# Half rows of the mixing two steps earlier between turned blocks, its last weights apart, VectorE's rests one step later

## The chip, the core and the metric

The kernel runs on one core of a Trainium2 chip. The metric is the device time in microseconds (us) of one execution. TensorE (PE in the profile) multiplies and transposes into the accumulation memory (PSUM), ScalarE (ACT) and VectorE (DVE) read it, GpSimd (POOL) and SyncE's queue (SP) stand beside them. TensorE works at one of two clock levels, 1.2 or 2.4 GHz; the profile shows the granted clock as a share of the higher one.

## The reference, cut to what matters

One layer of one model is followed by one layer of another, on 1024 tokens of width 1024, in float32. The change lies in the second layer, where a stick-breaking attention runs over 8 heads and the output of two attentions is mixed:

```python
oa = chunked_rel_attention(qa, ka, va, rel_bias)       # rows2[:, :, 0:512] in the kernel
ob = stick_breaking_attention(qb, kb, vb)              # rows2[:, :, 512:1024]
mixed = jnp.concatenate([rms_norm(oa) * g_a, rms_norm(ob) * g_b], axis=-1) @ w_out
x = x + gate_mix[:, None, :] * mixed
# stick_breaking_attention, for each block of 128 queries:
log_beta = jax.nn.log_sigmoid(logits)
log_keep = jnp.where(strict, jax.nn.log_sigmoid(-logits), 0.0)
log_tail = lax.cumsum(log_keep, axis=3, reverse=True) - log_keep
weights = jnp.where(strict, jnp.exp(log_beta + log_tail), 0.0)
outs.append(jnp.einsum("bhqk,bkhd->bqhd", weights, v))
```

The first half of the mixing, `rms_norm(oa) * g_a` with the upper 512 rows of `w_out`, needs only the attention that is already done; it can run beside the second attention.

## The kernel before

Every float32 product is made of three matmuls of rounded operands: high x high, low x high, high x low (`passes`, L818 to L820). So each operand exists as a high part, which ScalarE writes by a copy, and a low part, the **rest**, which VectorE writes by a subtraction.

The stick-breaking attention runs in 96 **steps** (`NS`), 24 for each of four pairs of heads. A step is one head, one block of 128 queries and up to four blocks of keys. Each engine has its own loop over `s`, and the order in it is written by hand:

- TensorE, step s: `turn3(s-2)` turns the weights (L1400), `outputs3(s-4)` multiplies them with v (L1416, L1418), `jobs3(s)` gives two slices of the q, k, v products of a coming pair (steps 0 to 71), `beside3(s)` follows, and in odd steps `scores3(s+1)` (L1385, L1391) gives the logits of the next two steps.
- ScalarE, step s: `turned_hi(s-3)` (wt_hi), `signs(s)` (keep, stick), the high part of a product that ended in step s-1 and the high part of the next weights (`stick_weight_hi`), `beside3(s)`.
- VectorE, step s: `tails(s-1)` (the scan L2452 over keep, the product L2456 with stick), `turned_lo3(s-3)` (wt_lo, L2461), the rest of that product (`job_lo`), `beside3(s)`, and last the rest of the next weights (`stick_weight_lo`, L2080).

`turn3(z)` waits for the tail of z and for the wt_lo two steps back. A product's half ends every fourth step, at s % 4 = 3; its rest stands in the step after. The table `BANK3` says which of the two banks of `pd[:, 0]` a product uses.

The mixing runs in `beside3`. **Blocks** 0 to 7 (`turn_mixed`) turn the first attention's output into `actT`, 128 columns by 512 rows each; blocks 8 to 11 do so for the first half of the rows of the second. **Half rows** 0 to 15 (`first_half_row`) multiply them with the first half of the weights, 12 matmuls each (row r = n // 2, half h = n % 2). VectorE's `first_half_sum(n)` scales the result (L2494, which frees the bank, `c0_free`) and adds it to the residual (L2497). The residual, `rows3`, comes back from DRAM by one DMA (L674) that SP issues when `outputs3(71)` has freed its place; the first sum waits for it (`mid_in`). ScalarE and VectorE split the eight tiles of mixing weights in steps 72 to 75 and 94 to 97 (`mix_weight_hi`, L1901, and `mix_weight_lo`, L2485). The second half of the mixing (`second_row`) starts when VectorE has left the loop.

Before, TensorE has blocks 0 to 7 in steps 74 to 77, two in each, half rows 0 to 15 in steps 78 to 93, and blocks 8 to 11 in steps 94 to 97; the other two engines follow one step later.

## Time and profile before

| | us |
|---|---|
| median of 3 timed runs | 2663.93 (2662.77 to 2664.50) |
| the profiled execution | 2653.37 |
| its span, from the first to the last instruction | 2651.6 |
| TensorE busy in the span | 2557.0 (96%) |
| VectorE busy | 1529.8 (58%) |
| ScalarE busy | 789.4 (30%) |
| TensorE's share of the chain that ended last | 87% |
| mean granted clock | 0.973 |

In the profile a row of the timeline tells the start, the busy time, engine and line, operation, output and inputs with their sizes, and the count; in square brackets stand the idle time before it and what ended that. Matmuls overlap, so what one costs is the distance from its start to the next start. The third attention lies between 1522 and 1856 us.

### The profile page before, as it was taken

The numbers are of one execution on the slowest core, as the hardware profiler recorded it, in microseconds if no ns is written. First come the engines' busy times: TensorE is split into PE (matmuls) and PEld (weight loads), VectorE is DVE, ScalarE is ACT, GpSimd is POOL, SyncE is SP. The second block draws the span as 40 slices with busy tenths as digits, with TensorE's granted clock in tenths as the row PEclk, the third lists the DMA queues.
The fourth block names the chain that finished last, engine by engine and source line by source line (L and its number), as shares of the span: only waits on it lengthen the run. The fifth ranks groups of instructions, "written<-read, shape, count | busy, mean of one in ns | idle before, by whom it ended". The sixth has DMA issues, their size and how long they took to land.

```text
span 2651.6 us, 32495 instructions
## 1 busy us (share of the span) xinstructions
PE 2557.0 (96%) x12496; PEld 2112.1 (80%) x12496; DVE 1529.8 (58%) x2345; ACT 789.4 (30%) x1353; POOL 188.4 (7%) x94
## 2 busy tenths in 40 slices
PE   7999999999999999998999999989999999999998
PEld 6777787888888888787888877777788888888886
DVE  6668265444344437646454577778566555646466
ACT  2245041111011102535433355544532121212122
POOL 6303300000000000001222200000000000000000
PEclk9996999999999999998999999979999999999999
DMA  3403613223232323113110001021012121202011
GB/s 121 37 9 81 79 33 93 93 77 94 86 93 77 94 86 117 31 42 116 32 42 27 25 17 33 17 96 38 19 56 64 33 63 32 63 32 63 32 56 72
DMA packets 201576, 157.05 MB, mean 59 GB/s; under 512 B 56184, under 2 KB 176512, under 8 KB 201472
## 3 DMA queue, kind: packets, MB, share of 16 engines
q1 hardware_dynamic: 183344, 124.94, 16.5%
q10 hardware_dynamic: 18128, 30.71, 4.4%
q8 instruction: 67, 1.10, 0.2%
q14 instruction: 37, 0.30, 0.0%
HBM read 147.23 MB, written 11.56 MB: 60 GB/s over the span
## 4 chain that ended last, share of the span: by engine, by line
PE 87%; DVE 6%; ACT 2%; issue 2%; DMA 2%; SPq 1%; POOL 1%; ACTq 0%; DVEq 0%; PEldq 0%; POOLq 0%
PE pd L818 25%; PE pd L820 25%; PE pd L819 25%; PE pt L1338 1%; PE pd L1385 1%; DMA raw<-in_w_out 1%; PE pd L1307 1%; PE pt L1400 1%; PE pt L818 1%; PE pt L1416 1%; PE pt L1355 1%; PE pt L838 1%; PE pt L1418 1%; PE pt L820 1%; PE pt L819 1%
## 5 line engine op out<-in xcount | busy, mean ns | idle before, releaser
L818 PE MATMUL pd<-actT_hi,st_hi 128*128 128x512 f32 x1872 | 749.3, 400 | 7.0 <-DVE st_lo L2233 3.6
L820 PE MATMUL pd<-actT_hi,st_lo 128*128 128x512 f32 x1872 | 733.4, 392 | 0.0
L819 PE MATMUL pd<-actT_lo,st_hi 128*128 128x512 f32 x1872 | 732.6, 391 | 0.0
L818 PEld LDWEIGHTS pd<-actT_hi,st_hi 128*128 128x128 f32 x1872 | 354.0, 189 | 76.9 <-ACT evac L1573 3.9
L820 PEld LDWEIGHTS pd<-actT_hi,st_lo 128*128 128x128 f32 x1872 | 353.2, 189 | 75.2
L819 PEld LDWEIGHTS pd<-actT_lo,st_hi 128*128 128x128 f32 x1872 | 354.4, 189 | 66.6
L818 PE MATMUL pd<-mv_hi,hid_hi 128*128 128x512 f32 x864 | 337.3, 390 | 3.5 <-DVE acc L2547 1.5
L819 PE MATMUL pd<-mv_lo,hid_hi 128*128 128x512 f32 x864 | 336.5, 389 | 0.0
L820 PE MATMUL pd<-mv_hi,hid_lo 128*128 128x512 f32 x864 | 336.3, 389 | 0.0
L1704 ACT ACTIVATE mv_hi<-raw 128x1024 fp32r<-128x1024 f32 x54 | 55.9, 1056 | 603.6 <-PE pd L820 478.1
L1573 ACT ACTIVATE evac<-pd 128x1024 f32<-128x1024 f32 x76 | 77.9, 1024 | 451.9 <-PE pd L820 451.9
L2196 DVE TENSOR_TENSOR acc<-acc,pd 128x1024 f32<-128x1024 f32 x72 | 87.9, 1221 | 190.9 <-PE pd L820 190.8
L818 PEld LDWEIGHTS pd<-mv_hi,hid_hi 128*128 128x128 f32 x864 | 162.2, 188 | 39.2 <-DVE acc L2547 3.2
L820 PEld LDWEIGHTS pd<-mv_hi,hid_lo 128*128 128x128 f32 x864 | 162.2, 188 | 33.8
L819 PEld LDWEIGHTS pd<-mv_lo,hid_hi 128*128 128x128 f32 x864 | 162.2, 188 | 33.3
L2233 DVE TENSOR_TENSOR st_lo<-raw,st_hi 128x1024 fp32r<-128x1024 f32 (+1 forms) x83 | 103.5, 1249 | 117.4 <-ACT st_hi L1704 111.2
L757 POOL TENSOR_TENSOR st_hi<-raw,ones 128x1024 fp32r<-128x1024 f32 x27 | 67.7, 2507 | 1186.9 <-PE pd L820 1170.3
L2546 DVE TENSOR_TENSOR gated<-pd,row_b 128x1024 f32<-128x1024 f32 x48 | 58.8, 1225 | 104.2 <-PE pd L820 103.5
L2606 DVE TENSOR_SCALAR cv<-evac,cw,cb 128x1024 f32<-128x1024 f32 x44 | 35.7, 811 | 119.0 <-ACT evac L1573 117.8
L1704 ACT ACTIVATE st_hi<-raw 128x1024 fp32r<-128x1024 f32 (+1 forms) x83 | 89.0, 1075 | 51.3 <-DMA raw<-in_w_ff 19.6
L2452 DVE TENSOR_TENSOR_SCAN tail<-keep,tail 128x512 f32<-128x512 f32 (+3 forms) x96 | 97.1, 1011 | 7.6 <-ACT keep L1874 7.1
L2233 DVE TENSOR_TENSOR mv_lo<-raw,mv_hi 128x1024 fp32r<-128x1024 f32 x54 | 65.0, 1223 | 60.4 <-ACT mv_hi L1704 59.1
(340 smaller groups left out, 3763.0 us busy)
## 6 DMA issues: line engine op xcount, KB each, us to landing
raw<-in_w_ff SPq DMA_DIRECT2D x64, 512.0 KB, 4.0
ada_raw<-in_w_ada ACTq DMA_DIRECT2D x64, 384.0 KB, 3.2
raw<-in_w_up SPq DMA_DIRECT2D x44, 512.0 KB, 3.8
raw<-in_w_in SPq DMA_DIRECT2D x30, 512.0 KB, 3.7
raw<-in_w_down SPq DMA_DIRECT2D x22, 512.0 KB, 3.4
acc<-in_x SPq DMA_DIRECT2D x16, 512.0 KB, 8.8
raw<-in_w_out SPq DMA_DIRECT2D x12, 512.0 KB, 3.4
raw<-in_w_ple_gate SPq DMA_DIRECT2D x8, 512.0 KB, 3.8
```

The costliest lines, as they stand in the source:

```text
L757: pool.tensor_tensor(hi.rearrange("p (k n) -> p k n", n=P), src.rearrange("p (k n) -> p k n", n=P), ones[:, :].unsqueeze(1).to_broadcast([ ...
L818: pe.matmul(out_ap, a_hi, b_hi, start=start, stop=False, skip_group_check=check)
L819: pe.matmul(out_ap, a_hi, b_lo, start=False, stop=False, skip_group_check=check)
L820: return pe.matmul(out_ap, a_lo, b_hi, start=False, stop=stop, skip_group_check=check)
L838: last = pe.transpose(pt[:, job % 4, r * P:(r + 1) * P], src[:, half * 4 + r, kt * P:(kt + 1) * P], ident[:, :])
L1573: act.activation(buf[:, t % 2, :], pd[:, t % 2, :], func, **kw).then_inc(t_free, 1)
L1704: act.activation(hi, src, ACT.Copy).then_inc(split_hi, 1)
L2196: return dve.tensor_tensor(acc[:, r, :], acc[:, r, :], pdr(r), ALU.add)
L2233: dve.tensor_tensor(lo, src, hi.bitcast(F32), ALU.subtract).then_inc(w_ready, 1)
L2452: link(dve.tensor_tensor_scan(tail[:, f % 2, c1 - n:c1][:, ::-1], kept, kept, tail[:, f % 2, c1:c1 + 1], ALU.mult, ALU.min))
L2546: link(dve.tensor_tensor(gt[:, :], pdr(r), row_gate[:, :], ALU.mult))
L2606: link(dve.tensor_scalar(y, u, cw[:, 2, ds(f, 1)], cb[:, ds(f, 1)], ALU.mult, ALU.add))
```

## The change

A table `mix_steps(s)` says which half rows ("r") and blocks ("b") a step has, and all three engines read it. Blocks 0 to 3 stay in steps 74 and 75. Half rows 0 to 15 stand in steps 76 to 91, and blocks 4 to 7 behind half rows 0 to 3, one in each. Blocks 8 to 11 stand in steps 92 to 95. `mix_bank` puts half rows 0 to 3 in bank 0 and blocks 4 to 7 in bank 1; the waits on `c0_free` and `tp_lo` follow from that. The last four mixing weights are split in steps 92, 93, 95 and 96, behind the step's block on ScalarE and VectorE. The rests of q and k products and of the attention's next weights stand one step later on VectorE.

```diff
+        def mix_steps(s):
+            if 74 <= s < 76:
+                return [("b", 2 * (s - 74)), ("b", 2 * (s - 74) + 1)]
+            if 76 <= s < 80:
+                return [("r", s - 76), ("b", s - 72)]
+            if 80 <= s < 92:
+                return [("r", s - 76)]
+            return [("b", s - 84)] if 92 <= s < 96 else []
+        def mix_bank(kind, n):
+            return 1 if kind == "b" and 4 <= n < 8 else 0 if kind == "r" and n < 4 else n % 2
...
             def first_half_row(n):
                 r, h = n // 2, n % 2
+                bank = mix_bank("r", n)
                 if n == 0:
                     pe.wait_ge(w_ready, UN["out2"] + 4)
+                    pe.wait_ge(tp_lo, TPJ["o2"] + 4)
+                elif n == 5:
                     pe.wait_ge(tp_lo, TPJ["o2"] + 8)
-                if n >= 2:
-                    pe.wait_ge(c0_free, n - 1)
+                else:
+                    pe.wait_ge(c0_free, n if n < 5 else n - 1)
...
-                if 94 <= s < 98:
-                    mix_weight_hi(s - 90)
-                if 95 <= s < 99:
-                    b = s - 87
-                    mixed_hi(b, pd[:, 0, b % 2 * HB:(b % 2 + 1) * HB])
+                if s in (92, 93, 95, 96):
+                    mix_weight_hi((92, 93, 95, 96).index(s) + 4)
...
-                    for q, e, kind, half in stick_ends(s - 1):
-                        job_lo(0, 4 * NJ1 + NJ2 * q, att2[q % 2], [(e, kind, half)], q)
+                    for q, e, kind, half in stick_ends(s - 1) + stick_ends(s - 2):
+                        if (kind == "T") == ((q, e, kind, half) in stick_ends(s - 1)):
+                            job_lo(0, 4 * NJ1 + NJ2 * q, att2[q % 2], [(e, kind, half)], q)
...
-                    for q, e, kind, half in stick_ends(s - 1):
+                    for q, e, kind, half in stick_ends(s - 2):
                         if kind != "T" and half:
                             stick_weight_lo(next_unit(q, e))
```

**VectorE, steps 16 and 17** (tail, stick: the tail and its product; k_lo2b: the rest of the k product; rsq: the inverse roots, 14 rows of which the first or last ones stand; st_lo: the rest of the next weights). Before, in two pieces:

```order
1355 L2461 TENSOR_TENSOR wt_lo<-pt,wt_hi 128x512
1356 L2097 TENSOR_TENSOR k_lo2b<-pd,k_hi2b 128x512
1357 L2467 TENSOR_SCALAR rsq_v<-ssq 128x8
1358 L2468 TENSOR_SCALAR rsq_a<-rsq_v 128x8
...
1370 L2473 TENSOR_TENSOR rsq_a<-rsq_a,rsq_t 128x8
1371 L2080 TENSOR_TENSOR st_lo<-raw,st_hi 128x1024
1372 L2452 SCALAR_TENSOR_TENSOR tail<-keep,tail 128x512
1373 L2456 TENSOR_TENSOR stick<-stick,tail 128x512
1374 L2461 TENSOR_TENSOR wt_lo<-pt,wt_hi 128x256
```

Now:

```order
1355 L2476 TENSOR_TENSOR wt_lo<-pt,wt_hi 128x512
1356 L2482 TENSOR_SCALAR rsq_v<-ssq 128x8
1357 L2483 TENSOR_SCALAR rsq_a<-rsq_v 128x8
...
1369 L2488 TENSOR_TENSOR rsq_a<-rsq_a,rsq_t 128x8
1370 L2467 SCALAR_TENSOR_TENSOR tail<-keep,tail 128x512
1371 L2471 TENSOR_TENSOR stick<-stick,tail 128x512
1372 L2476 TENSOR_TENSOR wt_lo<-pt,wt_hi 128x256
1373 L2112 TENSOR_TENSOR k_lo2b<-pd,k_hi2b 128x512
1374 L2095 TENSOR_TENSOR st_lo<-raw,st_hi 128x1024
```

The tail and the wt_lo that stood behind roots, k_lo2b and st_lo now stand directly behind the roots, ahead of the other two.

**TensorE, step 76 and the start of step 77** (L1400, now L1414: turned weights; ident,rows: blocks; w_hi, w_lo with actT: a half row; k, q: scores). Before:

```order
5278 L1400 MATMUL pt<-ident,stick 128x128 x2
5279 L1416 MATMUL pt<-v2b,wt_hi 128x128
5280 L1418 MATMUL pt<-v2b,wt_lo 128x64
5281 L1429 MATMUL pd<-ident,rows_56 128x128 x8
5282 L1400 MATMUL pt<-ident,stick 128x128 x2
5283 L1416 MATMUL pt<-v2b,wt_hi 128x128
5284 L1418 MATMUL pt<-v2b,wt_lo 128x64
5285 L1429 MATMUL pd<-ident,rows_56 128x128 x8
5286 L1385 MATMUL pd<-k_hi2b,q_hi2b 128x512 x2
```

Now:

```order
5278 L1414 MATMUL pt<-ident,stick 128x128 x2
5279 L1430 MATMUL pt<-v2b,wt_hi 128x128
5280 L1432 MATMUL pt<-v2b,wt_lo 128x64
5281 L832 MATMUL pd<-w_hi,actT_hi 128x512
5282 L833 MATMUL pd<-w_lo,actT_hi 128x512
...
5292 L834 MATMUL pd<-w_hi,actT_lo 128x512
5293 L1443 MATMUL pd<-ident,rows_56 128x128 x4
5294 L1414 MATMUL pt<-ident,stick 128x128 x2
5295 L1430 MATMUL pt<-v2b,wt_hi 128x128
5296 L1432 MATMUL pt<-v2b,wt_lo 128x64
5297 L832 MATMUL pd<-w_hi,actT_hi 128x512
```

Where two blocks of four transposes stood (x8), half row 0 stands with block 4 behind it, and half row 1 follows in the next step.

**VectorE, around the end of the half rows** (half_gated: the first operation of a sum; w_lo: a mixing weight's rest; actT_lo: a block's rest). Before, steps 94 and 95, with row 15's sum at the head:

```order
1675 L2494 SCALAR_TENSOR_TENSOR half_gated<-pd,rsq_a,mix_gate 128x512
1676 L2497 TENSOR_TENSOR rows_57<-rows_57,half_gated 128x512
1677 L2485 SCALAR_TENSOR_TENSOR w_lo<-raw,gab,w_hi 128x1024
1678 L2452 SCALAR_TENSOR_TENSOR tail<-keep,tail 128x512
1679 L2456 TENSOR_TENSOR stick<-stick,tail 128x512
1680 L2461 TENSOR_TENSOR wt_lo<-pt,wt_hi 128x512
1681 L2485 SCALAR_TENSOR_TENSOR w_lo<-raw,gab,w_hi 128x1024
1682 L2479 TENSOR_TENSOR actT_lo<-pd,actT_hi 128x512
1683 L2452 SCALAR_TENSOR_TENSOR tail<-keep,tail 128x512
```

Now, from row 15's sum in step 92:

```order
1671 L2509 SCALAR_TENSOR_TENSOR half_gated<-pd,rsq_a,mix_gate 128x512
1672 L2512 TENSOR_TENSOR rows_57<-rows_57,half_gated 128x512
1673 L2500 SCALAR_TENSOR_TENSOR w_lo<-raw,gab,w_hi 128x1024
1674 L2467 SCALAR_TENSOR_TENSOR tail<-keep,tail 128x512
1675 L2471 TENSOR_TENSOR stick<-stick,tail 128x512
1676 L2476 TENSOR_TENSOR wt_lo<-pt,wt_hi 128x384
1677 L2494 TENSOR_TENSOR actT_lo<-pd,actT_hi 128x512
1678 L2500 SCALAR_TENSOR_TENSOR w_lo<-raw,gab,w_hi 128x1024
1679 L2467 SCALAR_TENSOR_TENSOR tail<-keep,tail 128x512
1680 L2471 TENSOR_TENSOR stick<-stick,tail 128x512
1681 L2476 TENSOR_TENSOR wt_lo<-pt,wt_hi 128x384
1682 L2494 TENSOR_TENSOR actT_lo<-pd,actT_hi 128x512
```

The same weights and blocks follow row 15's sum; they now stand in steps with two more tails behind them, and the block comes ahead of the weight.

## Rows read from the trace of the kernel before

**Rows 1.** Stretches: us, busy PE, PEld, DVE, ACT, POOL (instructions), granted clock, DMA, GB/s

```profile
1574.40:1577.80 3.40, 3.40 (x14) 2.92 (x13) 3.37 (x6) 1.14 (x4) 0.00 (x0) 0.50 0.00 0
...
1745.00:1766.80 21.80, 16.46 (x72) 14.09 (x72) 15.52 (x27) 12.27 (x27) 0.00 (x0) 0.50 0.71 266
...
1766.80:1772.30 5.50, 5.44 (x13) 4.21 (x14) 2.26 (x3) 0.44 (x1) 0.00 (x0) 0.50 0.00 0
...
1772.40:1840.30 67.90, 67.90 (x403) 55.42 (x401) 56.42 (x80) 25.21 (x59) 0.00 (x0) 1.00 0.00 1
```

**Rows 2.** TensorE's timeline, turned weights of steps 10, 18, 42 and 43

```profile
1546.21 0.63 PE L1400 MATMUL pt<-ident,stick 128*128 128x128 f32 x4 [0.87 <-DVE wt_lo L2461]
...
1572.89 0.63 PE L1400 MATMUL pt<-ident,stick 128*128 128x128 f32 x4 [2.85 <-DVE wt_lo L2461]
...
1647.42 0.63 PE L1400 MATMUL pt<-ident,stick 128*128 128x128 f32 x4 [0.36 <-DVE wt_lo L2461]
...
1649.73 0.60 PE L1400 MATMUL pt<-ident,stick 128*128 128x128 f32 x4
```

**Rows 3.** VectorE's timeline, step 16

```profile
1565.83 0.69 DVE L2097 TENSOR_TENSOR k_lo2b<-pd,k_hi2b 128x512 fp32r<-128x512 f32 x1 [2.48 <-ACT k_hi2b L1609]
...
1569.26 1.22 DVE L2080 TENSOR_TENSOR st_lo<-raw,st_hi 128x1024 fp32r<-128x1024 f32 x1
...
1570.41 1.28 DVE L2452 TENSOR_TENSOR_SCAN tail<-keep,tail 128x512 f32<-128x512 f32 x1
```

**Rows 4.** TensorE's timeline, steps 78 to 82

```profile
1766.86 0.77 PE L818 MATMUL pd<-w_hi,actT_hi 128*128 128x512 f32 x1 [1.51 <-DVE actT_lo L2479]
...
1772.11 0.61 PE L1400 MATMUL pt<-ident,stick 128*128 128x128 f32 x3
...
1772.93 0.47 PE L818 MATMUL pd<-w_hi,actT_hi 128*128 128x512 f32 x1
...
1777.02 0.62 PE L1400 MATMUL pt<-ident,stick 128*128 128x128 f32 x4
...
1778.07 0.48 PE L818 MATMUL pd<-w_hi,actT_hi 128*128 128x512 f32 x1
...
1780.91 0.60 PE L1400 MATMUL pt<-ident,stick 128*128 128x128 f32 x4
...
1785.35 0.66 PE L1400 MATMUL pt<-ident,stick 128*128 128x128 f32 x4
```

**Rows 5.** SP's timeline and the DMA view (count, size, us to landing), residual

```profile
1749.93 0.38 SPq L674 DMA_DIRECT2D rows<-x_mid  x1
...
rows<-x_mid SPq DMA_DIRECT2D x1, 4096.0 KB, 14.0
```

**Rows 6.** VectorE's timeline, rests of blocks 2, 3 and the first sum

```profile
1755.70 1.29 DVE L2479 TENSOR_TENSOR actT_lo<-pd,actT_hi 128x512 fp32r<-128x512 f32 x2 [2.87 <-ACT actT_hi L1894]
...
1772.41 0.75 DVE L2494 SCALAR_TENSOR_TENSOR half_gated<-pd,rsq_a,mix_gate 128x512 f32<-128x512 f32 x1 [3.31 <-issue]
```

**Rows 7.** TensorE's timeline, steps 92 and 94, first row of the second half

```profile
1828.24 0.52 PE L1400 MATMUL pt<-ident,stick 128*128 128x128 f32 x3
...
1837.22 0.66 PE L1400 MATMUL pt<-ident,stick 128*128 128x128 f32 x4
...
1838.30 0.66 PE L1429 MATMUL pd<-ident,rows 128*128 128x128 f32 x4
...
1856.04 0.76 PE L818 MATMUL pd<-w_hi,actT_hi 128*128 128x512 f32 x1 [1.41 <-DVEq L2541]
```

**Rows 8.** VectorE's timeline, steps 92, 94 and 95

```profile
1830.95 0.55 DVE L2461 TENSOR_TENSOR wt_lo<-pt,wt_hi 128x384 fp32r<-128x384 f32 x1
...
1839.55 1.28 DVE L2485 SCALAR_TENSOR_TENSOR w_lo<-raw,gab,w_hi 128x1024 fp32r<-128x1024 f32 x1 [1.64 <-ACT w_hi L1901]
...
1840.75 1.28 DVE L2452 TENSOR_TENSOR_SCAN tail<-keep,tail 128x512 f32<-128x512 f32 x1
...
1842.67 0.69 DVE L2461 TENSOR_TENSOR wt_lo<-pt,wt_hi 128x512 fp32r<-128x512 f32 x1
```

More of the change, by code:

```diff
@@ L1433, in first_half_row @@
                 r, h = n // 2, n % 2
+                bank = mix_bank("r", n)
                 if n == 0:
                     pe.wait_ge(w_ready, UN["out2"] + 4)
+                    pe.wait_ge(tp_lo, TPJ["o2"] + 4)
+                elif n == 5:
                     pe.wait_ge(tp_lo, TPJ["o2"] + 8)
-                if n >= 2:
-                    pe.wait_ge(c0_free, n - 1)
+                else:
+                    pe.wait_ge(c0_free, n if n < 5 else n - 1)
                 for j in range(4):
-                    last = passes(pd[:, 0, h * HB:(h + 1) * HB], actT_hi[:, j, r * P:(r + 1) * P],
+                    last = passes(pd[:, 0, bank * HB:(bank + 1) * HB], actT_hi[:, j, r * P:(r + 1) * P],
                                   actT_lo[:, j, r * P:(r + 1) * P], w0_hi[:, j, h * HB:(h + 1) * HB],
@@ L1445, in beside3 @@
             def beside3(s):
-                if 74 <= s < 78:
-                    for b in range(2 * (s - 74), 2 * (s - 73)):
-                        if b < 2:
-                            pe.wait_ge(jb_lo, 4 * NJ1 + NL2 * 8)
-                        else:
-                            pe.wait_ge(tp_lo, TPJ["o2"] + b - 1)
-                        turn_mixed(b, pd[:, 0, b % 2 * HB:(b % 2 + 1) * HB])
-                elif 78 <= s < 94:
-                    first_half_row(s - 78)
-                elif 94 <= s < 98:
-                    b = s - 86
-                    if b == 8:
+                for kind, n in mix_steps(s):
+                    bank = mix_bank(kind, n)
+                    if kind == "r":
+                        first_half_row(n)
+                        continue
+                    if n < 2:
+                        pe.wait_ge(jb_lo, 4 * NJ1 + NL2 * 8)
+                    elif n == 4:
+                        pe.wait_ge(tp_lo, TPJ["o2"] + 4)
+                    elif 4 < n < 8:
+                        pe.wait_ge(tp_lo, TPJ["o2"] + n)
+                    elif n == 8:
                         pe.wait_ge(o_rows, 14)
                         pe.wait_ge(c0_free, 16)
-                    elif b >= 10:
-                        pe.wait_ge(tp_lo, TPJ["o2"] + b - 1)
-                    turn_mixed(b, pd[:, 0, b % 2 * HB:(b % 2 + 1) * HB])
+                    else:
+                        pe.wait_ge(tp_lo, TPJ["o2"] + n - 1)
+                    turn_mixed(n, pd[:, 0, bank * HB:(bank + 1) * HB])
             scores3(0)
@@ L1915, in beside3 @@
                     mix_weight_hi(s - 72)
-                if 75 <= s < 79:
-                    for b in range(2 * (s - 75), 2 * (s - 74)):
-                        mixed_hi(b, pd[:, 0, b % 2 * HB:(b % 2 + 1) * HB])
+                for kind, n in mix_steps(s - 1):
+                    bank = mix_bank(kind, n)
+                    if kind == "b":
+                        mixed_hi(n, pd[:, 0, bank * HB:(bank + 1) * HB])
                 if 88 <= s < 92:
@@ L2504, in beside3 @@
                     mix_weight_lo(s - 72)
-                if 75 <= s < 79:
-                    for b in range(2 * (s - 75), 2 * (s - 74)):
-                        mixed_lo(b, pd[:, 0, b % 2 * HB:(b % 2 + 1) * HB])
-                if 79 <= s < 95:
-                    if s == 79:
-                        dve.wait_ge(mix_gate_in, 16)
-                    first_half_sum(s - 79)
+                for kind, n in mix_steps(s - 1):
+                    bank = mix_bank(kind, n)
+                    if kind == "b":
+                        mixed_lo(n, pd[:, 0, bank * HB:(bank + 1) * HB])
+                    else:
+                        if n == 0:
+                            dve.wait_ge(mix_gate_in, 16)
+                        first_half_sum(n)
                 if s == 99:
```

10 lines of the change are left out of this document (3 added, 7 removed).

## The prediction

> **What bounds the kernel now.** I read the page first (its table stands above): TensorE is busy for 96% of the span and carries 87% of the chain that ended last, so only two things can move the end: idle time of TensorE, and time in which it works at the lower of its two clock levels, 1.2 instead of 2.4 GHz. Then I read the third attention, steps 0 to 99 at 1522 to 1856 us, by stretches with the granted clock, and looked up TensorE's gaps in its timeline. The reader is to see three kinds of loss. First, in steps 0 to 71 TensorE waits only now and then for VectorE, for the low part of the turned weights (wt_lo) [rows 2]; just before, VectorE had itself waited 2.48 us for ScalarE's high part of a product, with the next tail standing behind it in its order [rows 3]. Second, 1745 to 1766.8 is granted 0.50 and TensorE works 16.46 of 21.8 us: turned blocks without rows [rows 1, 4]. Third, the light steps at the end, where VectorE is full: 16.5 us without a gap from its fifth weight rest to the first row of the second half [rows 7, 8]. In between, 1772.4 to 1840.3, TensorE is full at full clock [rows 1]: there two half rows earlier are no gain in themselves, they only move work.
>
> **Part A, VectorE's rests one step later.** Nothing is added: 12 rests and 7 weight rests change places with one tail and one wt_lo. What it buys is the wait: in the step after a product ends, ScalarE has the keep and stick activations ahead of the high part. Worst is step 16, where the inverse roots stand there too. Before: wait to 1565.83, rest and roots to 1569.26, weight rest to 1570.41, and only then the tail; TensorE, ready at 1572.89 - 2.85 = 1570.04, starts at 1572.89 [rows 2, 3], and 1574.4 to 1577.8 is granted 0.50 [rows 1]. After: VectorE is free at 1565.83 - 2.48 = 1563.35 and starts with the roots (1569.26 - 1565.83 less the rest's 0.6 = 2.8) to 1566.2. ScalarE's keep for the tail is there, since it precedes the high part that came at 1565.8. Tail and product 1.92 (1840.75 to 1842.67 [rows 8]) to 1568.1, wt_lo 0.4 (tail, product, wt_lo and the hand-over are 2.48, 1570.41 to 1572.89) to 1568.5: TensorE waits for nothing at 1570.04. Rest 0.6, weight 1.15, tail 1.92, wt_lo 0.4 follow, to 1572.5; TensorE wants them one step later, 1570.04 + 2.3 (step 42, the same step of the next pair, 1647.42 to 1649.73 [rows 2]) = 1572.35, so some 0.2 is late next. The clock's dip follows this stall and should go with it; 3.4 us at half clock cost 1.7. Gain 2.85 - 0.2 + 1.7 = 4.35. The gap of 0.87 stands three times, once in each pair (steps 10, 34, 58) [rows 2] (there the first of them); there only rest and weight rest are in the way, and what is late next is the tail one step on, between 0 and 0.4. I take 0.75 of each, 2.25. The 0.36 of step 42 gives 0.3. The weights' loads leave SP's queue one step later too; they are wanted some eight steps later, so that costs nothing. **A = 6.9 us gained**; bounds 0 (the tail is late by as much) and 2.85 + 1.7 + 2.6 + 0.36 = 7.5.
>
> **Part B, rows 0 to 5 and blocks 4 to 7, up to step 82.** Steps 74 and 75 are as before. Row 0 needs the rests of blocks 0 to 3; their end is 1755.70 + 1.29 = 1757.0 [rows 6]. It runs at half clock as before, 5.25 us [rows 4], to 1762.3, block 4 (some 0.5: 0.66 less its overlap [rows 7]) and the small products of step 77 to 1763.3. Row 1 goes to the same bank and waits for VectorE's first sum, and this waits for the rows of x that come back from DRAM: issued at 1749.93 + 14.0 = 1763.9 [rows 5]. Before, that landing was hidden, row 0 ended at 1772.11; **now it ends last**. The sum's first operation 0.75 [rows 6], so row 1 starts at 1764.85, after a wait of 1.5. Then at full clock: row 1 and scores 4.09 (step 79 before is 4.91, less the 0.82 of its small products), block 0.5 = 4.6; step 78: 0.82 + 2.84 (a row alone, 1778.07 to 1780.91) + 0.5 = 4.15; step 79: 4.91 + 0.5 and some 0.4 of waiting for the sum in the single bank = 5.8; steps 80 and 81: 8.33 as 1777.02 to 1785.35 [rows 4]. Step 82 starts at 1764.85 + 22.9 = 1787.7 with six rows done, before at 1785.35 with four. Two rows are 5.7, the lag is 2.3: gain 3.4. Against it: the stretch around row 1 has a wait of 1.5 with 1 us of small work on either side, like the 2.85 with small work ahead of the dip of 1574.4 [rows 1, 2]. I take a dip of that size, 3.4 us at half clock, -1.7. **B = 1.7 us gained**, bounds 3.4 and, with the clock low to the end of row 3, -7.7 (below).
>
> By the Trainium skill ("TensorE: Matmul & The Clock Gate", section "Wait — 56ns, not 53.3ns?") matmuls of 512 columns start every 426.7 ns at 1.2 GHz and every 215.7 ns at 2.4. The first agrees with the trace (12 in 5.25 us). By the second two rows would be worth 24 x 0.2157 = 5.2 us instead of 5.7, and B half a microsecond less; the trace has 0.237 per matmul of a row, and the sum goes by that.
>
> **Part C, the last steps.** From the start of step 92 to the first row of the second half it takes 1856.04 - 1828.24 = 27.8 us before, of which rows 14 and 15 are 5.7: 22.1 [rows 7]. Now the light steps are 92 to 99 instead of 94 to 99. VectorE's first weight rest comes 2.3 us after the start of its step (1839.55 against 1837.22) [rows 7, 8], then its 16.5 us without a gap, and in them now two more tails (2 x 1.92) and two more wt_lo (2 x 0.5 [rows 8]): 2.3 + 16.5 + 4.85 = 23.7. The order of weights and blocks changes nothing in that sum; weights 6 and 7 land long before steps 95 and 96. The last outputs, which run at half clock here, end some 0.5 later than that by my estimate: 24.2. **C = -2.1 us.** Moving the rows forward takes them from under VectorE's cover here; that is where part of B goes back. Bounds: -2.1 - 1, if the weights wait behind ScalarE, and 0 if VectorE is not full in steps 92 and 93.
>
> **Sum**: 6.9 + 1.7 - 2.1 = 6.5, say 6.6 us gained by the profiled execution: 2653.37 - 6.6 = 2646.8. That execution is 10.6 us below the median of the timed runs, 2663.93; no row says where they spend more, so I take the difference over: 2657.3.
>
> **Rivals.** *The stall only moves on* (A falls): VectorE has as much to do as before, and if the tail of the next step is late by what was won, A is 0 to 1 and B + C = -0.4: 2663.5. For it: ScalarE still holds wt_hi behind weight and high part. Against it: VectorE idles 2.48 us right at the worst place [rows 3]. 0.20. *The clock stays low over the first rows* (slower): four rows share one bank, row 1 waits for the landing, and if TensorE is not granted 2.4 GHz before row 4, rows 1 to 3 cost 3 x (5.25 - 2.84) = 7.2 more, their blocks 3 x 0.5 = 1.5, scores and small products 2.4: 11.1 in place of 1.7, so 2657.3 + 9.4 = 2666.7; together with the first rival 2673. It decides at the end of row 0: before, the clock came back only when row 0 had run alone for 5.5 us [rows 1, 4]. Against it: row 0 and block 4 are 5.7 us again. 0.08. *No dip at all*: B is 3.4, and one of the short dips behind the stage (1.7) may fail to come, as they hang on stalls of 2 to 3 us: 2657.3 - 3.4 = 2653.9. 0.14. My forecast, with 0.58, has a range of its own of 2654.5 to 2660.5.
>
> **How the numbers follow.** What a measurement of this kernel tells from no change is 0.2%, 5.3 us: below 2658.6 is faster. Of the forecast three quarters lie below, 0.43; with 0.14 of the third rival 0.57 for faster. The rest of the forecast, the first rival and half of the second make 0.39 for no difference, and 0.04 is left for slower. Range 2653 to 2665: it leaves out the deeper ends of the second and third rival.
>
> **What would show it.** A: no gap at step 18, a granted clock of 1.00 at 1574 to 1578, and step 20 some 4 us earlier; wrong if the gap stands at step 19. B: row 1 starting right after the landing of the rows of x, about 15 us after their issue, and the granted clock back at row 1 or 2; wrong if rows 2 and 3 run in 5 us each. C: some 24 us from step 92 to the first row of the second half, VectorE without a gap; wrong if it is 22. The forecast as a whole is wrong if the landing comes much later than 14 us, or if the timed runs stall elsewhere than the profiled one.

## The result and the profile after

The changed kernel's timed runs have a median of 2647.48 us (20 runs), the kernel before beside them 2663.90 (20 runs). The ratio is 0.9946, with a 95% interval of 0.9932 to 0.9961: 14.4 us faster, 10.4 to 18.1. The forecast was 2657.3 with a range of 2653 to 2665, so the direction is right and the time lies below the range. A second measurement of the same kernel (10 runs) gave 0.9967 (0.9949 to 0.9985), 8.8 us. Weighting the two by their intervals gives 0.9954, 12.2 us (about 9 to 15). The profiled execution took 2644.14 us, its span 2642.3. One timed run of the kernel pool_weights below took 3198.04 us, some 20% more than its others, and stands in no ratio.

The page of the changed kernel: busy time of the engines, and the chain that ended last by engine. The answering numbers of before stand in its table (TensorE 2557.0, 96%, and 87% of the chain).

```profile
PE 2558.7 (97%) x12496; PEld 2112.3 (80%) x12496; DVE 1530.6 (58%) x2345; ACT 788.6 (30%) x1353; POOL 189.5 (7%) x94
...
PE 89%; DVE 5%; ACT 2%; DMA 2%; issue 2%; POOL 1%; SPq 0%; ACTq 0%; DVEq 0%; PEldq 0%; POOLq 0%
```

The span is 9.3 us shorter, but that is not the measure of the change: the changed kernel's execution starts the third attention 3.8 us later (step 8 at 1543.48 against 1539.67), where nothing was changed, because its clock was low for 88.7 us of the first 410 against 68.2. So I measure by stretches between starts on TensorE. Each number is a difference of two starts in the timeline; some of the rows that enter are shown here or in [rows 4, 7]. (12.1 us are gained in these stretches and 3.8 lost ahead of them; the last 1.0 of the 9.3 lies behind them, where the kernel before has a dip of the clock of 3.4 us at 1919.1 that this trace lacks. It stands in eight of the fourteen traces read here, with either order.)

| us | before | after | difference |
|---|---|---|---|
| A: step 8 to step 72 | 198.63 | 189.21 | 9.4 gained |
| B: step 72 to step 83 | 51.21 | 51.53, with two rows (5.7) more | 5.4 gained |
| step 83 to step 92 | 38.73 | 38.73 | 0 |
| C: step 92 to the second half's first row | 27.80 | 24.77, with two rows (5.7) fewer | 2.7 lost |
| sum | 316.37 | 304.24 | 12.1 gained |

The forecasts were A 6.9, B 1.7, C -2.1. The order's three places look as follows.

**A.** TensorE's timeline of the changed kernel at the places of [rows 2], the turned weights of steps 10, 18, 42 and 43, and of step 11:

```profile
1549.07 0.66 PE L1414 MATMUL pt<-ident,stick 128*128 128x128 f32 x4
...
1552.30 0.63 PE L1414 MATMUL pt<-ident,stick 128*128 128x128 f32 x4 [0.28 <-DVE wt_lo L2476]
...
1572.98 0.66 PE L1414 MATMUL pt<-ident,stick 128*128 128x128 f32 x4
...
1643.66 0.66 PE L1414 MATMUL pt<-ident,stick 128*128 128x128 f32 x4
...
1645.99 0.60 PE L1414 MATMUL pt<-ident,stick 128*128 128x128 f32 x4
```

VectorE's timeline there in steps 16 and 17, to set beside [rows 3]:

```profile
1565.32 0.69 DVE L2476 TENSOR_TENSOR wt_lo<-pt,wt_hi 128x512 fp32r<-128x512 f32 x1
...
1568.75 1.28 DVE L2467 TENSOR_TENSOR_SCAN tail<-keep,tail 128x512 f32<-128x512 f32 x1
...
1571.01 0.68 DVE L2112 TENSOR_TENSOR k_lo2b<-pd,k_hi2b 128x512 fp32r<-128x512 f32 x1
...
1571.61 1.22 DVE L2095 TENSOR_TENSOR st_lo<-raw,st_hi 128x1024 fp32r<-128x1024 f32 x1
```

No wait is left in front of the four steps. One has come, 0.28 us in front of step 11: the tail behind the moved rest is late there, as the forecast had allowed for. VectorE goes from the turned weights straight to the roots, which end at 1568.75, takes the tail, and only then k_lo2b, whose high part has long been there: the 2.48 us of waiting of [rows 3] are gone. Part of A is seen in full only on TensorE's weight loads (PEld); of the matmul rows behind them two carry a wait, of 0.31 and 0.32 us. The weight loads' timeline in the kernel before shows five such waits; two of them, in steps 29 and 37:

```profile
1608.08 0.19 PEld L1416 LDWEIGHTS pt<-v2b,wt_hi 128*128 128x128 f32 x1 [0.55 <-DVE rows L2535]
...
1632.71 0.19 PEld L1416 LDWEIGHTS pt<-v2b,wt_hi 128*128 128x128 f32 x1 [0.46 <-DVE rows L2535]
```

Here the outputs wait for VectorE's add of the heads' rows (L2535), which frees their bank. The changed kernel has none of the five.

**B.** The answers to [rows 4 to 6]. TensorE's timeline of the changed kernel, at half row 0, block 4, half rows 1 and 3:

```profile
1751.55 0.47 PE L832 MATMUL pd<-w_hi,actT_hi 128*128 128x512 f32 x1 [2.32 <-DVE actT_lo L2494]
...
1755.97 0.60 PE L1443 MATMUL pd<-ident,rows 128*128 128x128 f32 x4
...
1757.07 0.50 PE L832 MATMUL pd<-w_hi,actT_hi 128*128 128x512 f32 x1
...
1767.18 0.50 PE L832 MATMUL pd<-w_hi,actT_hi 128*128 128x512 f32 x1 [0.72 <-DVE half_gated L2509]
```

SP's timeline, the issue of the residual's load:

```profile
1743.17 0.38 SPq L688 DMA_DIRECT2D rows<-x_mid  x1
```

The DMA view (issues, KB, us to landing):

```profile
rows<-x_mid SPq DMA_DIRECT2D x1, 4096.0 KB, 13.0
```

VectorE's timeline, its first sum:

```profile
1756.26 0.75 DVE L2509 SCALAR_TENSOR_TENSOR half_gated<-pd,rsq_a,mix_gate 128x512 f32<-128x512 f32 x1 [2.67 <-PE pd L834]
```

**The clock.** Stretches of the changed kernel, columns as in [rows 1]:

```profile
1574.40:1577.80 3.40, 3.40 (x21) 2.63 (x21) 3.37 (x6) 1.78 (x4) 0.00 (x0) 1.00 0.47 142
1741.80:1748.60 6.80, 4.88 (x24) 3.98 (x22) 5.34 (x10) 2.56 (x5) 0.00 (x0) 0.50 0.62 210
1748.70:1752.00 3.30, 0.98 (x7) 0.86 (x8) 1.88 (x4) 2.90 (x7) 0.00 (x0) 1.00 1.02 421
1752.10:1755.50 3.40, 3.40 (x9) 2.67 (x8) 1.46 (x3) 0.00 (x0) 0.00 (x0) 0.50 1.03 413
1755.60:1830.50 74.90, 72.33 (x434) 59.00 (x433) 62.39 (x89) 31.04 (x70) 0.00 (x0) 1.00 0.06 20
1830.60:1851.10 20.50, 15.45 (x64) 13.96 (x63) 15.89 (x33) 7.19 (x12) 0.00 (x0) 0.50 0.33 104
```

At 1574.4 the granted clock is 1.00, it was 0.50. Around the first rows it is low for 6.8 + 3.4 = 10.2 us, before for 21.8 + 5.5 = 27.3 [rows 1]; row 0 runs at half clock only until 1755.5 and takes 4.42 us (5.25 before). Row 1 follows 1.1 us later, behind block 4 and the small products. Its matmul row carries no wait (its weight load 0.25 us, for the sum), since the load landed at 1743.17 + 13.0 = 1756.2, just when row 0 was done: VectorE's first sum had waited for TensorE last, not for the load.

**C.** TensorE's timeline of the changed kernel, turned weights of steps 92, 95 and 97 and the second half's first row, as in [rows 7]:

```profile
1822.95 0.52 PE L1414 MATMUL pt<-ident,stick 128*128 128x128 f32 x3
...
1833.26 1.09 PE L1414 MATMUL pt<-ident,stick 128*128 128x128 f32 x4 [2.37 <-DVE wt_lo L2476]
...
1840.68 1.08 PE L1414 MATMUL pt<-ident,stick 128*128 128x128 f32 x4 [1.68 <-DVE wt_lo L2476]
...
1847.72 0.76 PE L832 MATMUL pd<-w_hi,actT_hi 128*128 128x512 f32 x1 [1.00 <-DVEq L2555]
```

VectorE's timeline, its first weight rest and tail, and the last two wt_lo, as in [rows 8]:

```profile
1825.26 1.28 DVE L2500 SCALAR_TENSOR_TENSOR w_lo<-raw,gab,w_hi 128x1024 fp32r<-128x1024 f32 x1 [1.88 <-ACT w_hi L1918]
...
1826.46 1.28 DVE L2467 TENSOR_TENSOR_SCAN tail<-keep,tail 128x512 f32<-128x512 f32 x1
...
1842.25 0.68 DVE L2476 TENSOR_TENSOR wt_lo<-pt,wt_hi 128x512 fp32r<-128x512 f32 x1
...
1844.04 0.69 DVE L2476 TENSOR_TENSOR wt_lo<-pt,wt_hi 128x512 fp32r<-128x512 f32 x1 [1.11 <-ACT wt_hi L1901]
```

VectorE has its first weight rest at 1825.26, 2.3 us after the start of step 92, and works from there to 1842.9 without a gap, with TensorE waiting for its wt_lo. Ahead of its last wt_lo it waits 1.11 us for ScalarE; in the kernel before VectorE has no gap here.

### The profile page after: what moved, and what is told of

It is laid out like the page before. It is cut to its first block, busy times and chain, and to the rows that moved or that the text cites. A ratio compares the mean times of both kernels' runs of the same rounds, so it can differ in the third digit from the quotient of the medians.

```text
span 2642.3 us, 32495 instructions
## 1 busy us (share of the span) xinstructions
PE 2558.7 (97%) x12496; PEld 2112.3 (80%) x12496; DVE 1530.6 (58%) x2345; ACT 788.6 (30%) x1353; POOL 189.5 (7%) x94
## 4 chain that ended last, share of the span: by engine, by line
PE 89%; DVE 5%; ACT 2%; DMA 2%; issue 2%; POOL 1%; SPq 0%; ACTq 0%; DVEq 0%; PEldq 0%; POOLq 0%
PE pd L832 26%; PE pd L834 25%; PE pd L833 25%; PE pt L1352 1%; PE pd L1399 1%; PE pt L1414 1%; PE pt L1430 1%; PE pd L1321 1%; PE pt L832 1%; DMA raw<-in_w_out 1%; PE pt L1369 1%; PE pt L1432 1%; PE pt L852 1%; PE pt L833 1%; PE pt L834 1%
```

## The experiments

**The theory**: A, B and C as measured above, and they add up. **The rivals**: the surplus over the forecast lies outside these steps (in the timed runs' clock), or in one of the parts alone. Since single times of one kernel scatter by some 7 us (standard deviation of the changed kernel's 20), a mean over 12 is good to 2 us, over 6 to 3; the stretches between steps repeat to 0.1 us where the clock is the same. So each run is read by both. Each time stands against 20 to 35 runs of the kernel before that were measured beside it.

| run | runs | time against before (95%) | A: 8 to 72 | B: 72 to 83 | 92 to row |
|---|---|---|---|---|---|
| before | 20 to 35 | 1 | 198.63 | 51.21 | 27.80 |
| changed | 20 | 0.9946 (0.9932 to 0.9961) | 189.21 | 51.53 | 24.77 |
| changed, again | 10 | 0.9967 (0.9949 to 0.9985) | 189.19 | 52.66 | 24.78 |
| rests_alone | 12 | 0.9979 (0.9957 to 1.0001) | 189.28 | 50.37 | 27.80 |
| step16_alone | 12 | 0.9967 (0.9946 to 0.9988) | 194.43 | 51.54 | 27.79 |
| adds_first | 1 | - | 196.43 | 47.37 | 28.54 |
| mix_alone | 12 | 0.9985 (0.9961 to 1.0009) | 198.62 | 53.68 | 24.77 |
| load_late | 12 | 0.9979 (0.9959 to 0.9999) | 189.29 | 61.04 | 24.78 |
| load_split | 1 | - | 189.24 | 51.50 | 24.78 |
| pool_weights | 11 | 0.9962 (0.9942 to 0.9983) | 189.23 | 51.52 | 25.09 |
| both | 12 | 0.9941 (0.9920 to 0.9962) | 189.20 | 51.45 | 25.10 |
| late_weights | 10 | 0.9962 (0.9945 to 0.9978) | 189.22 | 51.47 | 24.29 |
| early_split | 6 | 0.9940 (0.9923 to 0.9958) | 189.22 | 51.63 | 24.78 |
| combined | 12 | 0.9947 (0.9925 to 0.9969) | 189.25 | 51.59 | 24.28 |

**1. The rests alone.** The kernel before with this on VectorE:

```diff
-                    for q, e, kind, half in stick_ends(s - 1):
-                        job_lo(0, 4 * NJ1 + NJ2 * q, att2[q % 2], [(e, kind, half)], q)
+                    for q, e, kind, half in stick_ends(s - 1) + stick_ends(s - 2):
+                        if (kind == "T") == ((q, e, kind, half) in stick_ends(s - 1)):
+                            job_lo(0, 4 * NJ1 + NJ2 * q, att2[q % 2], [(e, kind, half)], q)
...
-                    for q, e, kind, half in stick_ends(s - 1):
+                    for q, e, kind, half in stick_ends(s - 2):
                         if kind != "T" and half:
                             stick_weight_lo(next_unit(q, e))
```

> The kernel before with VectorE's rests one step later and nothing else (part A alone). My theory, from the two traces: A is worth 9.4 us, not the 6.9 forecast: 4.5 at steps 16 to 20 and at every later pair 0.9 for the tail, and beside them 0.4 to 0.6 each time for the outputs, which no longer wait for VectorE's rows add. Time 2663.9 - 9.4 = 2654.5; the start of step 72 about 9.4 us earlier against the third attention's own start, no wait of outputs for rows. The rival, that the sum of the forecast was right and the rest of the 16 us came from elsewhere: 6.9 us, 2657. Another rival, that A is worth more in the timed runs than in a profiled one because stalls bring dips of the clock: 2650 or less.

A is 198.63 - 189.28 = 9.35, as in the changed kernel, and C is as before. The timed 5.6 us (interval from 0 to 11) hold 9.4 and also 6.9; they can't choose between them, the trace does.

**2. The mixing alone.** The changed kernel with these two edits taken back.

> The changed kernel with VectorE's rests where they stood before (parts B and C alone). My theory: B is 5.4 gained, C is 2.65 lost, together 2.75: 2661.1, and the two parts add up to the change. In the trace: from the start of step 72 to step 82 about 5.4 us less than before with two more rows done, low clock for some 10 us in place of 27. The rival: the surplus of the timed runs (14 to 16 us against 12 in the traces) comes from here, since a shorter stretch with light steps keeps the clock up in more runs: 5 to 7 gained, 2657 to 2659. The forecast's B + C, -0.4: 2664.3.

The timed 4.0 us (interval from -2 to 10) again can't choose, and with the 5.6 of the rests alone they make 9.6. In the trace A is nought and C is -2.7 again (27.80 - 5.7 - 24.77). B came out 51.21 + 5.7 - 53.68 = 3.2, less than the 5.4 expected. The reason is in two rows of this run. VectorE's timeline, the first sum:

```profile
1768.46 0.75 DVE L2509 SCALAR_TENSOR_TENSOR half_gated<-pd,rsq_a,mix_gate 128x512 f32<-128x512 f32 x1 [4.86 <-DMA rows<-x_mid]
```

TensorE's timeline, half row 1:

```profile
1769.27 0.53 PE L832 MATMUL pd<-w_hi,actT_hi 128*128 128x512 f32 x1 [1.55 <-DVE half_gated L2509]
```

The load came last here, landed 13.9 us after its issue at 1754.44, and row 1 waited 1.55 us for the sum behind it, after 17.1 us of low clock. This is the course that the forecast had described (a wait of 1.5 us), without the second dip that it had put behind it. The changed kernel's second profile shows the same in small: landed after 13.9 us, row 1 waited 1.10, and B is 4.3.

**3. Step 16 alone.** The kernel before, with rest and weight rest of step 16 in step 17; all others stay.

```diff
-                    for q, e, kind, half in stick_ends(s - 1):
+                    for q, e, kind, half in stick_ends(15 if s == 17 else s - 1 if s != 16 else -1):
```

> The kernel before with only the rest of the k product and of the weight of step 16, beside the inverse roots, one step later; the other pairs are left. My theory: the stall of 2.85 us at step 18, its dip of the clock and nothing else go, 4.2 to 4.5 gained, 2659.5; the waits of 0.87 and of 0.36 to 0.6 stay. The rival, that the clock's dip is no consequence of this stall (another comes a little later): 2.5 gained, 2661.4.

198.63 - 194.43 = 4.2. (The timed 8.8 us, 3 to 14, are more than the 5.6 of the run that holds this edit and all the others: times can't tell such parts apart.) The dip of the clock goes with the stall: of the fourteen traces, the three that keep the stall of 2.85 us (before, mix_alone, adds_first) have 3.4 us of low clock 1.5 us behind it, the eleven without it have none there.

**4. The add ahead of the rest.** The kernel before, one exchange on VectorE: the add to the heads' rows stands ahead of the product's rest of its step.

```diff
+                g = half_ended(s - 5)
+                if g is not None:
+                    out_rows, o = rows3_of(g)
+                    dve.wait_ge(o_cp, g + 1)
+                    dve.tensor_tensor(out_rows, out_rows, o[:, :, 64:P], ALU.add).then_inc(o_rows, 1)
                 if 1 <= s <= 3 * NB + 2:
                     for q, e, kind, half in stick_ends(s - 1):
                         job_lo(0, 4 * NJ1 + NJ2 * q, att2[q % 2], [(e, kind, half)], q)
                 beside3(s)
-                g = half_ended(s - 5)
...
```

> The kernel before with one exchange on VectorE: the add of the heads' outputs to their rows stands ahead of the product's rest in its step, not behind it. It tests where the part of A that the forecast lacked comes from. My theory: the five waits of the outputs for that add (0.36 to 0.6 us each, at steps 13, 29, 37, 53 and 61) go, steps behind them start 2.2 us sooner in all, and the waits of 0.87, 2.85 and 0.36 for the low part of the turned weights stay as they are. The rival, that the rests' own place is the cause and the add is held back by the tail ahead of it: no change of those waits, 0. Read from the trace; 2 us can't be told in single times.

198.63 - 196.43 = 2.2, as expected. In this run's timeline of the weight loads step 29 has no wait:

```profile
1617.25 0.19 PEld L1416 LDWEIGHTS pt<-v2b,wt_hi 128*128 128x128 f32 x1
```

and on TensorE the stall of step 18 stands:

```profile
1582.60 0.63 PE L1400 MATMUL pt<-ident,stick 128*128 128x128 f32 x4 [2.85 <-DVE wt_lo L2461]
```

So 2.2 us of A come from adds that had stood behind a rest that waited for ScalarE, and the rest's delay did both. (Its B, 47.37, is the best of all that don't have the changed mixing: the clock was low for 13.7 us only. More on this below. Its last column, 28.54, is 0.7 worse than before's, and that is this edit's own doing: from step 92 to step 97 it takes 19.58 us in both, but at the end an add now stands ahead of the inverse roots and waits 0.33 us for ScalarE.)

**5. The load one step later**, on the changed kernel:

```diff
-                    sp.wait_ge(b_pv, 3 * NB)
+                    sp.wait_ge(b_pv, 3 * NB + 1)
```

> The changed kernel with the load of the residual's rows issued one step later, behind the outputs of step 76 in place of those of step 75. Against the changed kernel. In the trace of the changed kernel the load lands within 0.1 us of the moment when row 0 ends and the first sum can start, so there is no slack: issued 8 us later (1751.4 for 1743.2) it lands 8 us later and row 1 starts 8 us later, at 1765, some 8 us lost, and about 1.7 to 4 more where the clock goes low for it: 10 us slower than the changed kernel. The rival, that VectorE's first sum has slack behind it (rows 1 to 3 could catch up): 4 us or less.

B is worse by 61.04 - 51.53 = 9.5. Counted from the start of step 72 the load was issued 6.1 us later than in the changed kernel, not the 8 I had expected, and took 14.2 us for 13.0, so it landed 7.3 us later, at 1756.4. TensorE's timeline of this run, half row 1:

```profile
1757.36 0.79 PE L832 MATMUL pd<-w_hi,actT_hi 128*128 128x512 f32 x1 [7.43 <-DVE half_gated L2509]
```

So there is no slack: in the changed kernel the load lands when it is wanted. 7.4 us of the 9.5 are the wait; the rest goes with a stretch of low clock, 1755.2 to 1762.0, that the changed kernel does not have.

**6. The load in two parts**, on the changed kernel: rows 0 and 1 first, each part with its own semaphore.

```diff
-                    sp.dma_start(rows3[:, :, :], x_mid.rearrange("(r p) n -> p r n", p=P)).then_inc(mid_in, 16)
+                    for g, rs in enumerate((slice(0, 2), slice(2, 8))):
+                        sp.dma_start(rows3[:, rs, :], x_mid.rearrange("(r p) n -> p r n", p=P)[:, rs, :])\
+                            .then_inc(mid_in[g], 16)
...
-                if n == 0:
-                    dve.wait_ge(mid_in, 16)
+                if n in (0, 4):
+                    dve.wait_ge(mid_in[n // 4], 16)
```

> The changed kernel with the residual's one load cut in two, rows 0 and 1 (1 MB) first, the other six behind them, and the sums waiting for each at its first use. It tests whether the whole load of 4 MB is what row 1 waits for when the clock is low or the load slow (13.0 to 14.3 us so far; row 1 waited 1.55 us in the run with the mixing alone). My theory: the first part lands in 4 to 6 us, the first sum never waits for it, and B, from step 72 to step 82 with two rows more, is 4.9 to 5.4 us better than before. The rival, that both parts are served side by side and land together: 13 to 14 us for the first, B 3.2 to 5.4 as without.

The DMA view of this run has both parts:

```profile
rows<-x_mid SPq DMA_DIRECT2D x1, 3072.0 KB, 12.3
...
rows<-x_mid SPq DMA_DIRECT2D x1, 1024.0 KB, 4.9
```

The first part lands 4.9 us after its issue. All four runs with the load in two have 51.45 to 51.63 in B's column, the two (early_split, combined) whose second part took 13.6 us among them. So none of the four shows the 1 to 2 us that mix_alone and the changed kernel's second trace lose by the load, and nothing is gained where the load was in time.

**7. The weights' rests on GpSimd**, on the changed kernel:

```diff
                 act.activation(hi, src, ACT.Copy, scale=gab[:, c:c + 1]).then_inc(split_hi, 1)
+                if c >= 4:
+                    act.wait_ge(split_hi, n)
+                    act.activation(src, src, ACT.Copy, scale=gab[:, c:c + 1]).then_inc(w_scaled, 1)
...
+            for c in range(4, 8):
+                hi, lo, src, _, _, n = unit_of("out2", None, c)
+                pool.wait_ge(w_scaled, c - 3)
+                pool.tensor_tensor(lo, src, hi.bitcast(F32), ALU.subtract).then_inc(w_ready, 1)
```

> The changed kernel with the rests of the last four mixing weights taken from VectorE: ScalarE scales the weight in place with a second copy and GpSimd subtracts the high part. It tests whether C is VectorE's queue. My theory: VectorE has 4 x 1.15 = 4.6 us less in the steps from 92 on, and from the start of step 92 to the first row of the second half it takes 24.8 - 4 = 20.8 us, 4 us faster than the changed kernel. Rival 1, that the chain of turned weights between ScalarE, VectorE and TensorE bounds these steps and not VectorE's work: 1 us or less. Rival 2, that GpSimd's subtraction of 2.5 us each slows VectorE beside it or ends last: no gain or a loss, the second half waits for the weights.

From step 92 to the row it takes 25.09 in place of 24.77: 4.6 us of VectorE's work gone, and nothing gained. GpSimd's timeline in this run shows the third of its subtractions:

```profile
1828.86 2.94 POOL L828 TENSOR_TENSOR w_lo<-raw,w_hi 128x1024 fp32r<-128x1024 f32 x1 [3.44 <-ACT raw L1926]
```

and VectorE's two products, one in front of it and one beside it:

```profile
1826.57 0.69 DVE L2479 TENSOR_TENSOR stick<-stick,tail 128x512 f32<-128x512 f32 x1
...
1829.68 2.67 DVE L2479 TENSOR_TENSOR stick<-stick,tail 128x512 f32<-128x512 f32 x1
```

The product with stick, 0.69 us otherwise, took 2.67 us beside GpSimd's subtraction, to 1832.35; the subtraction's row ends at 1831.80. Besides, ScalarE's second copies stand ahead of wt_hi and actT_hi, for which VectorE now waits 0.9 to 1.0 us three times. That is 2.0 + 2.8 = 4.8 us of new holdups, and step 97 starts 17.76 us after step 92 for 17.73. The fourth rest had stood behind the last tail; where it was, VectorE now waits for ScalarE, 2.31 us for 1.11. So the run shows the second rival, but it doesn't tell what less work on VectorE alone would give. **Both** (this and the load in two) ends at 25.10.

> The two last edits together on the changed kernel, as a candidate. My theory: 4 us from the weights and 0 to 2 from the load, 2644 against 2648.3 for the mean of the changed kernel's runs. The rival, with GpSimd in VectorE's way: no faster than the changed kernel.

**8. The weights' rests later**, on the changed kernel:

```diff
-                if s == 99:
+                if s == 92:
                     dve.wait_ge(ob_sq, 4)
                     inverse_roots(rsq_b[:, 0:4], ssq[:, 8:12], HB)
-                if s in (92, 93, 95, 96):
-                    mix_weight_lo((92, 93, 95, 96).index(s) + 4)
+                if s in (92, 93, 97, 98):
+                    mix_weight_lo((92, 93, 97, 98).index(s) + 4)
```

> The changed kernel with VectorE's work of the last steps in another order: the inverse roots for the second half's rows stand in step 92, where VectorE idles 1.9 us for ScalarE, not in step 99, and the rests of the last two mixing weights in steps 97 and 98, behind the last steps' tails. It tests C without GpSimd: if the tails queue behind VectorE's own work, two rests of 1.2 less ahead of them and 0.9 more of roots save 1.5 us, and the end of the loop 0 to 0.5 more: from step 92 to the first row of the second half 22.8 to 23.3 us instead of 24.8. The rival, as with GpSimd, that the steps are bound by the chain from engine to engine: 24.3 or more.

24.29, so 0.5 gained of the 1.5 to 2 expected. That is the rival's number, but the rows don't show the rival's reason. VectorE's timeline in this run, its first weight rest:

```profile
1842.55 1.28 DVE L2500 SCALAR_TENSOR_TENSOR w_lo<-raw,gab,w_hi 128x1024 fp32r<-128x1024 f32 x1
```

TensorE's timeline in this run, the turned weights of steps 94 and 97 and the first row of the second half:

```profile
1846.37 0.62 PE L1414 MATMUL pt<-ident,stick 128*128 128x128 f32 x4 [2.50 <-DVE wt_lo L2476]
...
1856.79 1.09 PE L1414 MATMUL pt<-ident,stick 128*128 128x128 f32 x4 [0.48 <-DVE wt_lo L2476]
...
1863.58 0.76 PE L832 MATMUL pd<-w_hi,actT_hi 128*128 128x512 f32 x1 [0.74 <-DVEq L2555]
```

The inverse roots take 2.8 us and don't fit into the 1.9 that VectorE idles in step 92: the first weight rest starts 3.26 us after the start of the step (at 1839.29), in the changed kernel 2.31, and step 94 starts 0.95 later, after a wait of 2.50 for 1.55. And only one of the two rests moved, 1.2 us, had stood ahead of the last tail; the other stood behind it. 1.2 - 0.95 = 0.25 is what VectorE's queue gives, and step 97 starts 0.23 sooner, its wait down to 0.48 from 1.68. From there to the row it is 6.8 us against 7.04, since the roots are gone from the end. So these steps follow VectorE's queue, as the forecast had it. Only 0.48 us are left at step 97 for a later rest to win; what the rests alone give, with the roots left in step 99, was not run.

**9. The changed kernel again, blocks sooner, and all together.** The blocks' edit, on the kernel with the load in two:

```diff
-            if 74 <= s < 76:
-                return [("b", 2 * (s - 74)), ("b", 2 * (s - 74) + 1)]
+            if 72 <= s < 74:
+                return [("b", s - 72)]
+            if s == 74:
+                return [("b", 2), ("b", 3)]
```

> The changed kernel once more, on the chip of the three that follow. Two questions. First, whether B (from step 72 to step 82, two rows more done) is 5.4 us better than the kernel before or varies with the clock: of the traces so far with the changed order and the early load three gave 5.4 and one, whose clock stayed low for 17 us, 3.2; with the order of before three gave -0.3 to 0.8 and one, low for only 14 us, 3.8. I expect 5.4 again, with some 10 us of low clock; the rival says that these steps gain nothing on the average and anything from 1 to 5.4 comes out. Second, the time: mean 2648 of 12 runs if what was measured first holds, 13.5 us below before; 2653 if the traces' minimum of 8 to 9 us is all.

> The kernel with the residual's load cut in two, and blocks 0 and 1 moved to steps 72 and 73, one in each, blocks 2 and 3 both in step 74. In the changed kernel TensorE waits 1.92 us in step 74 or 75 for a block's rest and 2.32 us ahead of row 0. Without the cut the load would be late (13 us), with it the first part lands 5 us after its issue, before row 0 ends. My theory: both waits go, row 0 starts 3 to 4 us sooner after the start of step 72 (13.2 us before, 9.5 to 10 now), and the clock is low for less: 3 to 5 us faster than the changed kernel. The rival, that these steps are bound by ScalarE and VectorE, which split four mixing weights there: the waits move on to the turned weights, 1 us or less.

> The cut load, the blocks sooner and the weights' rests later, all on the changed kernel, as a candidate to beat it: 1.5 to 2 and 3 to 5 us, 2642 against 2648 for the mean of the changed kernel. The rival: the changed kernel's time within 2 us.

The first gave 0.9967 and B = 4.3, between what I had expected and the rival. The blocks sooner changed nothing: 51.63. (The expectation's 13.2 us to row 0 is a slip; in the changed kernel it is 1751.55 - 1732.69 = 18.9, here 1760.84 - 1742.37 = 18.5.) The wait in front of row 0 is gone, but the block waits grew, as TensorE's timeline of early_split shows at blocks 1 and 3:

```profile
1748.92 1.11 PE L1447 MATMUL pd<-ident,rows 128*128 128x128 f32 x4 [2.88 <-DVE actT_lo L2500]
...
1755.57 0.69 PE L1447 MATMUL pd<-ident,rows 128*128 128x128 f32 x2 [1.11 <-DVE actT_lo L2500]
```

From step 72 to row 0 TensorE waits 2.88 + 1.11 = 4.0 us for blocks, where the changed kernel waits 1.91 + 1.92 + 2.32 = 6.2 (1740.56, 1745.06, 1751.55). Of these 2.2 us less of idle time only 0.4 reach row 0; the rest went into the same work at a lower clock, as the row of its clock shows:

```profile
1748.10:1765.20 17.10, 15.17 (x60) 12.70 (x61) 12.07 (x22) 8.35 (x19) 0.00 (x0) 0.50 0.43 156
```

The clock is low without a break for 17.1 us, to the end of row 0, where the changed kernel has 10.2 us with a stretch at full clock inside. In combined it is the same again (17.1 us low, 51.59). None of these kernels is faster than the changed one beyond the intervals.

## Why the prediction was wrong

**A: 9.4 for 6.9. The step that failed is the list of what VectorE's rests hold up.** It held only the waits of the turned weights for wt_lo. By steps, from the starts in both traces: step 18 gives 2.93 and steps 19 and 20 another 1.6, the late tail that I charged (0.2) did not show and the dip went: 4.5 for 4.35. The three gaps of 0.87 leave 0.43, 0.9 and 0.9 behind: 2.2 for 2.25. (I had allowed for a late tail of up to 0.4 at each; it came at the first alone, as the wait of 0.28 at step 11.) Step 42 gives 0.4 for 0.3. These terms were right. Missing are the five waits of the outputs (0.36, 0.58, 0.36, 0.59, 0.36, together 2.25), which stand in full only on the rows of TensorE's weight loads; I had read the waits of the turned weights alone. Run 4 confirms them, 2.2 by itself. The bound of 7.5 was no bound, as it summed only the waits on my list. The first rival, that the stall moves on, fell: no gap at 19, and 189.19 to 189.29 for A in all ten traces that have the rests one step later.

**B: 5.4 for 1.7 in the first profile, 3.2 to 5.4 over the traces. The mechanism was right, two sizes were off.** Shifted by A (5.61 us up to step 72), row 0 starts at 1751.55 + 5.61 = 1757.2, forecast 1757.0; the load is issued at 1748.8 for 1749.93 and takes 13.0 for 14.0, so it lands at 1761.8 for 1763.9; row 1 starts at 1762.7 for 1764.85, 2.2 sooner. The wait of 1.5 us for the landing, on which the forecast turned, is nought in the first profile and 1.10 and 1.55 in two others: which it is hangs on a load that takes 13.0 or 13.9 us. Row 3 waits 0.72 for the single bank, forecast 0.4. And the second dip, 1.7, did not come: not behind row 1's waits of 1.10 and 1.55 us either, only in load_late, within its wait of 7.43 and behind it. The forecast had charged it by likeness to the stall of 2.85. 2.2 - 0.3 + 1.7 = 3.6 is the surplus. I used the load's time from one row, 14.0, as a constant; over the runs with one load it is 12.8 to 14.3 us. The second rival, clock low over rows 1 to 3, did not happen in any trace with the load issued in time.

The table also shows what I took as fixed and is not: without the changed mixing B is 51.21, 51.54, 50.37 and 47.37 (the last in adds_first, where the adds stand elsewhere in these steps too). The difference goes with the clock, low for 27.3, 27.3, 17.0 (two stretches) and 13.7 us. So the gain of B against before's mean, 50.12, is 3.9 on the average of seven traces of the changed order (51.97; load_late and the two with the blocks sooner left out), and 5.4 holds only against the one trace of before that was there first. Without adds_first before's mean is 51.04, and the gain 4.8. With that, the change is worth 9.4 + 3.9 - 2.7 = 10.6 us (11.5 with the 4.8), 12.1 in the first pair of profiles; the timed 12.2 (9 to 15) holds them all.

**C: -2.7 for -2.1.** The place and the mechanism were right: VectorE full from its first weight rest, and two more tails and wt_lo. The sum for its queue comes out: 16.5 + 4.85 = 21.35 forecast, and from 1825.26 to the row at 1847.72 it is 22.46, of which 1.11 is the wait for ScalarE's last wt_hi. That wait is the term that was too small: the forecast had 0.5 for the last steps at half clock. The clock is now low from 1830.6, so for 17.1 us ahead of the second half's first row, before for 12.0 (1844.0 to 1856.04), and ScalarE waits ahead of that wt_hi for TensorE's outputs, which run at half clock. Run 8 confirms the queue (steps 94 and 97 move by what is put in front of them); run 7 put about as much into it as it took out.

**The transfer to the timed runs. This step failed too.** I took the profile's distance to the median, 10.6 us, over as if it belonged to the kernel. In the changed kernel it is 3.3 (2644.14 and 2647.48). Single executions scatter by 7 us, so each distance is the luck of one execution, and 7.2 of the 9.8 us between forecast and median come from here. The other 2.6 are the profiled execution's, 2644.14 for a forecast of 2646.8: 5.5 us more in the parts and 1.0 behind them, less the 3.8 lost ahead of them. Against the kernel before, where this term falls out, the first measurement's 14.4 is 2.2 over the 12.2 of both together, within its interval. Single runs of the changed kernel lie up to 29 us apart (2634.76 to 2663.50). Where such a spread can come from stands in the traces: step 2 of the third attention, ahead of all that was changed, starts between 1519.81 (both) and 1545.43 us (combined), and the clock was low for 61.4 and 102.4 us of their first 410. Another dip outside this stage, 17.1 us long from 1316 or 1324 on, stands in two of the fourteen traces. What decides these dips is left open.

## What to carry to other kernels

When an operation that waits for another engine is moved back in an in-order queue, list everything queued behind it, adds that free a bank included, and look at the weight-load rows as well as the matmul rows for who waits for them. Bound a gain at a stall together with the clock dip behind it, which here went with the stall in all fourteen traces, but charge no new dip by likeness. Where a full queue bounds light steps, work gives something only when it is moved behind the last operation that another engine waits for, and what is moved forward must fit the idle time there. Idle time saved can be taken back by the clock. Judge such edits by stretches between fixed steps over several profiles, since single times differ by more than the change, and don't carry one execution's distance to the median over to another kernel.
